# Order of four engines' work in steps 18 to 21 of an attention loop, Trainium2

## The reference

```python
def diff_attention(q1, q2, k1, k2, v, lam):
    p = probs(q1, k1) - lam * probs(q2, k2)        # causal softmax, per head
    o = einsum('bhqs,bshe->bqhe', p, v)
# second_block
o_a = dsa_attention(q_a, k_a, v_a, q_i, k_i, w_i)
o_d = diff_attention(q1, q2, k1, k2, v_d, lam)
o_d = rmsnorm(o_d, g_diff_sub) * (1.0 - lam_init)   # per head: the root and the division
mix = concatenate([o_a, o_d]); y = mix @ w_out
x = x + rmsnorm(y, g_post_mix)
```

## Time and profile before

| | |
|---|---|
| median of 3 runs | 1122.99 us (1122.48 to 1123.41) |
| profiled execution | 1123.0 us, of which span 1121.3 us |
| PE busy | 1111.1 us, 99% of the span |
| DVE, ACT, POOL busy | 703.5, 402.1, 681.8 us |
| granted TensorE clock | 0.999 of full speed |

### The profile page before, as it was taken

How to read it: one execution, slowest core, us unless ns; L and a number is a source line. 1 busy time by engine, 2 the same in 40 slices (tenths; PEclk the granted TensorE clock), 3 DMA queues, 4 the chain that set the end, 5 groups by cost and what they waited for, 6 DMA issues and landing times.

```text
span 1121.3 us, 17271 instructions
## 1 busy us (share of the span) xinstructions
PE 1111.1 (99%) x6173; PEld 942.9 (84%) x6173; DVE 703.5 (63%) x1377; ACT 402.1 (36%) x814; POOL 681.8 (61%) x460
## 2 busy tenths in 40 slices
PE   9999999999999999999999999999999999999997
PEld 7888888998889998888778777677899888999886
DVE  5999778850158853447789777666887113885023
ACT  5146566530015631120202346645665000554012
POOL 7879946686636686667456433225847763558662
PEclk9999999999999999999999999999999999999999
DMA  7421222342213343324342221112224822235411
GB/s 253 131 92 59 75 84 86 113 133 94 94 61 109 114 152 98 107 95 132 114 130 95 86 84 58 38 58 75 75 76 137 184 94 67 88 111 172 167 57 75
DMA packets 52251, 115.54 MB, mean 103 GB/s; under 512 B 21840, under 2 KB 22480, under 8 KB 52176
## 3 DMA queue, kind: packets, MB, share of 16 engines
q1 hardware_dynamic: 31200, 105.40, 29.0%
q10 hardware_dynamic: 20976, 9.15, 3.3%
HBM read 105.09 MB, written 4.19 MB: 97 GB/s over the span
## 4 chain that ended last, share of the span: by engine, by line
PE 97%; ACT 1%; DMA 0%; DVE 0%; SPq 0%; issue 0%; DVEq 0%; ACTq 0%
PE bank L749 21%; PE bank L751 21%; PE bank L750 20%; PE bank L1407 5%; PE bank L1406 5%; PE bank L1405 5%; PE bank L781 2%; PE bank L783 2%; PE bank L782 2%; PE bank L1240 2%; PE bank L807 1%; PE bank L1254 1%; PE bank L815 1%; PE bank L808 1%; PE bank L1282 1%; PE bank L1278 1%
## 5 line engine op out<-in xcount | busy, mean ns | idle before, releaser
L551 POOL TENSOR_TENSOR wl<-raw,wh 128x1024 fp32r<-128x1024 f32 x140 | 336.8, 2405 | 11.7
L548 POOL TENSOR_SCALAR wh<-raw 128x1024 fp32r<-128x1024 f32 x139 | 149.2, 1074 | 258.0 <-PE bank L751 143.5
L749 PE MATMUL bank<-xh,wh 128*128 128x512 f32 (+2 forms) x672 | 234.5, 349 | 0.0
L751 PE MATMUL bank<-xh,wl 128*128 128x512 f32 (+2 forms) x672 | 229.4, 341 | 0.0
L750 PE MATMUL bank<-xl,wh 128*128 128x512 f32 (+2 forms) x672 | 229.1, 341 | 0.0
L749 PEld LDWEIGHTS bank<-xh,wh 128*128 128x128 f32 x672 | 126.8, 189 | 29.0 <-issue 16.4
L1638 ACT ACTIVATE wh<-bank 128x512 fp32r<-128x512 f32 x96 | 52.2, 596 | 253.1 <-DVE bank L2295 109.6
L751 PEld LDWEIGHTS bank<-xh,wl 128*128 128x128 f32 x672 | 126.8, 189 | 14.3
L750 PEld LDWEIGHTS bank<-xl,wh 128*128 128x128 f32 x672 | 126.9, 189 | 12.7 <-issue 0.2
L749 PE MATMUL bank<-uh,wh 128*128 128x512 f32 x288 | 112.7, 391 | 0.0
L751 PE MATMUL bank<-uh,wl 128*128 128x512 f32 x288 | 112.1, 389 | 0.0
(11 more groups left out here) (366 smaller groups left out, 2284.3 us busy)
## 6 DMA issues: line engine op xcount, KB each, us to landing
raw<-wstream SPq DMA_DIRECT2D x188, 512.0 KB, 3.5
x<-xT SPq DMA_DIRECT2D x8, 256.0 KB, 4.9
x4rows<-x_rows ACTq DMA_DIRECT2D x4, 512.0 KB, 9.6
out<-x4rows SPq DMA_DIRECT2D x8, 256.0 KB, 2.1
qd<-ropey ACTq DMA_DIRECT2D x16, 64.0 KB, 2.1
kd<-ropey ACTq DMA_DIRECT2D x16, 64.0 KB, 2.1
qa<-ropey SPq DMA_DIRECT2D x16, 64.0 KB, 2.0
ka<-ropey SPq DMA_DIRECT2D x16, 64.0 KB, 2.0
```

Of the source, the lines that this page charges most:

```text
L548: nc.gpsimd.tensor_scalar(wh[c][:], raw[c][:], 1.0, 1.0, ALU.mult, ALU.mult).then_inc(high_ready, 1)
L551: nc.gpsimd.tensor_tensor(wl[c][:], raw[c][:], wh[c][:].bitcast(F32), ALU.subtract).then_inc(split_ready, 1)
L749: mm(out, wh_, mh, start=start, stop=False)
L751: return mm(out, wl_, mh, start=False, stop=stop)
```

## The change

It moves instructions within the steps and adds or removes none.

- ACT, step 18: the copies of the turned tile 18 stand in front of the heads' root, which stood at the end of step 17.
- PE, step 19: the third spread (10) stands behind `values(18)` rather than in front of it.
- PE, steps 20 and 21: the last spread (11) stands behind `scores(23)` in step 21; it stood between `turn(20)` and `values(19)` in step 20.
- DVE, step 19: `head_factors(1)` stands behind `shift(21)` rather than in front of it.
- DVE, steps 19 and 20: `rope_odd(9)`, the join, stands behind `normalise(20)`; it stood at the end of step 19, in front of that.
- The other edits give names to lines that stay where they are.

```diff
-LOW_AT = {20: 2, 21: 3}
@@ PE
                 if n + 2 < TILES:
                     scores(n + 2)
+                if n == 21:
+                    pe.wait_ge(xl_ready, 3 * KT + 3)
+                    norm_spread(11)
...
                     turn(n)
+                if n >= 1:
+                    values(n - 1)
                 if n in SPREAD_AT and SPREAD_AT[n] == 2:
                     pe.wait_ge(bc_used, 10)
                     norm_spread(10)
-                if n in SPREAD_AT and SPREAD_AT[n] == 3:
-                    pe.wait_ge(xl_ready, 3 * KT + 3)
-                    norm_spread(11)
-                if n >= 1:
-                    values(n - 1)
@@ ACT
                     keep_turned(n)
+                if n == 18:
+                    head_roots(17)
                 if n in HIGH_AT:
...
-                if n in (9, 17):
-                    head_roots(n)
+                if n == 9:
+                    head_roots(9)
@@ DVE
                     normalise(n)
-                if n in LOW_AT:
...
+                if n == 20:
+                    rope_odd(9, E_QK + 6)
+                    head_low(2)
+                if n == 21:
+                    head_low(3)
...
+                if n + 2 < TILES:
+                    shift(n + 2)
                 if n == 19:
                     head_factors(1)
-                if n + 2 < TILES:
-                    shift(n + 2)
...
-                if n == 19:
-                    rope_odd(9, E_QK + 6)
```

More of the change, by code:

```diff
@@ L1820, in head_roots, with head_high @@
                 A(sd[:, 0:8], NB[:, 0:8], ACT.Sqrt).then_inc(sd_ready, 1)
+            def head_high(h):
+                act.wait_ge(chunk_done, C_OUT2)
+                act.wait_ge(bc_used, 9 + h)
+                A(xh[:, 4 + h], kept[h][:] if h < 2 else NB[:], ACT.Copy).then_inc(xh_ready, 1)
             def step(n):
@@ L1824, in step @@
                     keep_turned(n)
+                if n == 18:
+                    head_roots(17)
                 if n in HIGH_AT:
[L1827 to L1830, removed]
+                    head_high(HIGH_AT[n])
                 ends_head = n % 4 == 0 and 1 <= n // 4 <= DIFF_HEADS
@@ L2638, in head_factors, with head_low @@
                 V.reciprocal(rn[:, 0:8], sd[:, 0:8]).then_inc(rn_ready, 2)
+            def head_low(h):
+                if h == 2:
+                    dve.wait_ge(xl_ready, 3 * KT + 2)
+                    lows[0] += 2
+                dve.wait_ge(xh_ready, lows[0] + 1)
+                V.tensor_tensor(xl[:, 4 + h], NB[:], xh[:, 4 + h].bitcast(F32), ALU.subtract).then_inc(xl_ready, 1)
+                lows[0] += 1
             def step(n):
```

## The result

| | before | after |
|---|---|---|
| median of 20 runs each | 1122.78 us (1122.40 to 1123.41) | 1124.49 us (1124.00 to 1126.62) |
| ratio, 95% interval | | 1.0018 (1.0012 to 1.0024) |
| profiled execution, span | 1123.0, 1121.3 us | 1124.28, 1122.5 us |
| PE busy | 1111.1 us | 1111.1 us |

The change makes the kernel slower by 1.7 us, 0.15% by the medians and 0.18% by the ratio: less than the 0.2% named in the prediction, more than its 1.2, and inside its range; the interval lies wholly above 1. Five of the twenty runs of after took 1125.7 to 1126.6 us and the others 1124.0 to 1125.0, which lifts the ratio above that of the medians; no trace shows why. PE's work is the same to 0.1 us; what grew is the time in which it stands.

What follows compares the result with a forecast made beforehand. PE, busy 1111.1 of 1121.3 us, bounds the kernel. Stalls removed 0.66 + 0.62 = 1.28, added 0.24 + 0.42 + 1.75 + 0.09 = 2.5: net +1.2 on 1123.0 gives 1124.2 us, range 1122.5 to 1125.2.

Steps and rivals of the forecast that it cites:

- both stalls: PE's waits before turn(19), 0.66 us, and before spread 11, 0.62 us; both predicted to go, 1.28 us removed.
- second half of turn(20), wait: PE, step 20: new stall of 0.24 us, waiting for ACT's second copy of tile 19.
- join's moves landed: SP's eight moves behind the join, pushed 1.0 us later, land at 708.6; scores(24) can't start before.
- the wait at scores(23): PE waits for the first half of DVE's shift(22), behind head 2's low part: new stall 0.42 us.
- The 0.1 that the root was to cost ACT's chain: ACT: with copies first, the exponential of tile 20 starts at 700.0 rather than 699.89, everything behind it 0.1 us later.
- The wait at piece 3: PE waits for head 3's low part, late because DVE runs product, normalise(21) and low part behind spread 11: 1.75 us.
- the moves end last: Rival: the join's moves hold scores(24) to about 708.65, 0.5 us late, 1123.5 us; chance 0.12.
- Both stalls gone with nothing in their place: Rival: PE's two stalls go and no new wait replaces them, 1121.8 us; chance 0.06.
- ACT's tables: Rival: ACT pays one more table's worth, 1.28 us, between copies, root and exponential, 1125.5 us; chance 0.07.
- the change does nothing: Rival: PE's first stall stays or spread 11 keeps its distance, 1123.0 us give or take 0.3; chance 0.05.

Runs made afterwards that it cites:

- the fifth run, run 5: The change with DVE's shift(22) in front of head 2's low part in step 20; distance from piece 0's second matmul to scores(24) 11.83 us (change 12.57).
- the fourth run: The change with DVE's normalise(21) in front of the product of head 3; distance from piece 0's second matmul to scores(24) 12.48 us (change 12.57).
- the sixth run: The change with the last spread between values(19) and scores(23); ratio 1.0003, distance to scores(24) 11.51 us (before 10.91).
- runs 1: The change with the last spread put back between turn(20) and values(19); ratio 1.0006, distance to scores(24) 11.51 us (before 10.91).
- runs 2: The change with the last spread put back and DVE's join in front of its wait for spread 10; ratio 1.0005, distance to scores(24) 10.91 us.
- run 7: The change with the last spread between values(19) and scores(23) and the join before DVE's wait for spread 10; ratio 0.9998, distance to scores(24) 10.70 us.
- the third run: The kernel before with only ACT's copies of tile 18 in front of the heads' root; ratio 1.0002, distance to scores(24) 10.91 us, as before.
- run 9: The kernel of run 7 with piece 3 moved behind turn(21); ratio 0.9996, distance to scores(24) 10.24 us (before 10.91).

## Why the prediction was right, and where its size was off

Its mechanism held: both stalls go, and the late spread makes piece 3 wait for head 3's low part by more than they cost. In two places its account was not right, the halves of scores(23) and what makes the low part late; both follow below the table. On the scale of before (after plus 0.37), with the prediction's times first:

| step | predicted | measured |
|---|---|---|
| turn(19) | 697.68, no wait | 697.68, no wait |
| spread 10 | 699.48 | 699.45 |
| scores(22) | 700.00 | 700.03 |
| second half of turn(20), wait | 0.24 | 0.12 |
| scores(23), wait | 0.42 | 0.41 for the first half and 0.47 for the second |
| spread 11 | 704.71 | 705.07 |
| piece 3, wait | 1.75 | 1.83 from where it was due |
| join's moves landed | 708.6 | 708.7 |
| scores(24) | 709.3 | 709.8 |

**The term that was mis-sized is the wait at scores(23).** The prediction counted only the first half of shift(22) and gave scores(23) its 1.06 from there, so that a second half ready 0.5 later cost nothing. That would hold if the halves followed one another. They run side by side: the four matmuls take 1.13 with both halves ready and 1.60 with the second late (703.17 above). That is 0.47 left out of the sum, and the fifth run, which takes most of it away, gives back 0.74 of the 0.88. The Trainium skill, "TensorEngine Tiling (Array Packing)", section "Key Properties", says that different tiles of the array can run matmuls in parallel; the halves here are 64-row tiles, and the trace agrees.

Two small terms. The 0.1 that the root was to cost ACT's chain didn't arrive, as ACT began the copies earlier (695.87, 696.24 on the scale of before, put at 696.35): the exponential of tile 20 starts at 699.52 + 0.37 = 699.89, as before; hence 0.12 at turn(20). And the first matmul of piece 3 takes 0.33 to the next (707.71 to 708.04), where right behind piece 2 it took 0.24. Together: 1.16 predicted for scores(24), plus 0.47 and 0.10, less 0.12, is 1.61; measured 1.66. That the time came nearer, 1124.49 against 1124.2, is luck: the forecast added its 1.2 to 1123.0, and the twenty runs of before have a median of 1122.78.

**The wait at piece 3** was put down to DVE's queue: product, division, low part. In the change they do follow one another without a gap (705.39 to 707.65), and the sum is right in time. But the fourth run shows that the queue is not what makes the low part late: without the division in it, ACT's high part fills the gap and 0.09 of the distance is won. That the sum fits is in part luck: of two chains nearly equal in length it followed one and left out the other. The cause is the late spread, shown by the first and the sixth run.

**The rivals.** That the moves end last does not hold for the change as it is, and holds as the floor the prediction gave (0.5 over before): 0.60 in runs 1 and 6, and gone with an early join in runs 2 and 7. That rival was to decide if the division of tile 21 came earlier; in the fourth run it came earlier, and piece 3 still waits 1.56. Both stalls gone with nothing in their place: no; the third run shows the first one's 0.66 given back within 6 us. ACT's tables: the loads are 1.28 each and the next instruction starts 0.02 behind (698.03, 699.52 above), with copies in front of one and the root in front of the other. For the drain of about 1.38 us that the Trainium skill gives ("ScalarE: Activation LUTs", "What ACT_TABLE_LOAD costs") there is no room in either place. That the change does nothing: no.

## What to carry to other kernels

Before moving an instruction out of a stall, follow what hangs on its result to the next point where the bounding engine needs it, and count the work that this engine still has in between: here that work fell from 3.5 to 1.2 us while the chain beside it needed 3. Two stalls behind one chain of another engine are one stall; removing the first moves its time to the second. And a transfer issued by a queue inherits every place that its producer is moved down: 0.5 us of cover was gone with a move of 1 us.

## What the runs showed of the hardware

Scores of 64 rows run two at a time: four matmuls of 512 columns take 1.13 us with both halves' banks free, and 1.27, 1.43 and 1.60 if the second half comes 0.15, 0.30 and 0.48 later (run 5, runs 6 and 7, the change). The first 512-column matmul of a piece takes 0.31 to 0.34 to the next start, with a wait in front of it (0.34 in run 7) or without one, behind scores (0.33 at piece 2 before, 705.74 to 706.07) or behind transposes (0.31 in run 9); right behind another piece it takes 0.24. The eight moves of 64 KB are issued about 0.63 apart and land 1.9 to 2.0 later in every run.
